# A two-layer hybrid decoder trunk on one core: the norm squares of the dilated blocks move from ScalarE to GpSimd and VectorE

## The chip, the cores and the metric

One core of one Trainium2 chip. The metric is the device time of the whole kernel in microseconds, one launch for both layers. The engines are TensorE (PE, its weight loads PEld), VectorE (DVE), ScalarE (ACT), GpSimd (POOL) and SyncE (SP), which issues the DMAs. Lines named L797 and the like are lines of the kernel before.

## The reference

256 tokens, D_MODEL 1024, two layers. Each layer normalizes x, multiplies it by one wide w_in (1024 rows) and gives parts of the product to three mixers: a latent attention (A), a gated DeltaNet (B) and a dilated window attention (C) with three groups of four heads of 128. Gated branch outputs are projected, merged and put through w_out. The change concerns C, where queries and keys are normalized per head before the rotary embedding:

```python
def rms_norm(x, g):
    xf = x.astype(jnp.float32)
    y = xf * lax.rsqrt(jnp.mean(xf * xf, axis=-1, keepdims=True) + RMS_EPS)
    return (y * g.astype(jnp.float32)).astype(x.dtype)
...
    q, k, v = (t.reshape(B, S, n_heads, DIL_HEAD_DIM) for t in jnp.split(qkv, 3, axis=-1))
    q = apply_rope(rms_norm(q, q_norm_g), cos, sin)
    k = apply_rope(rms_norm(k, k_norm_g), cos, sin)
```

## The kernel before

Everything is float32. Each product with weights is made of three TensorE passes over split operands: high part times high part, high times low, low times high (L797 to L799). The weights come by DMA in pieces of 128x1024 into `raw` (4 slots); ScalarE writes the high part (`prep`, L1119, `w_hi`), VectorE the low part (`prep`, L1446, `w_lo`), into 5 slots each, so that a piece can be made four pieces ahead of its use.

The work is a list of 57 units per layer (`UNITS`, built in `unit_list`), each half of one projection block of 512 columns: 4 row blocks of weights (2 pieces of 2) by 2 token tiles `t` of 128 tokens. A unit's token tile is 12 matmuls of 128x512. Between the units stand all other steps, in one order that is written out by hand (`step_table`, `middle_table`, `build_order`). Each engine walks through this same `ORDER` and emits its own part of each step; an engine's instructions run strictly in that order, and between engines there are only semaphore waits. Behind the second token tile of unit u come its eviction step `("evict", u)`, the steps of `put(u, ...)`, and `prep` of the pieces of unit u + 2.

The dilated blocks are `dil` i = 0 to 8: for group g = i // 3, the queries are i = 3g, the keys 3g + 1, the values 3g + 2. The second halves of the query and key blocks 0, 1, 3, 4, 6, 7 are units 17, 22, 26, 28, 32 and 34. For such a block:

1. TensorE fills two PSUM banks, one per token tile.
2. ScalarE's `evict` (L1121 to L1190) takes each tile: four squares, one per head (L1186, sums of squares into `d_part`), then one scaled copy into the staging tile `stg` (L1189), which frees the bank. `stg` may be overwritten when the rope step of the block before has ended.
3. GpSimd's `d_rs` (L2051) makes the inverse root from the sums.
4. VectorE's `d_rope` (L1787 to L1806) rotates `stg` into `gate`. For keys it first waits until the queries have been transposed out of `gate`, and the other way round.
5. GpSimd's `d_scale` (L2069 to L2075) multiplies `gate` by the roots, two operations of 128x512. The queries of group 0 are not scaled here.
6. TensorE's `tr_step` (L884) transposes the result, four transposes per token tile; ScalarE copies them out (L1362), and scores, softmax and the product with the values follow.

The entries of the order around these steps, shortened:

```python
    put(22, ("dn_cv", 2, 1), ("tr", "dq", 0), ("dn_row", 0), ("dn_row", 1), ("tr", "dq", 1), ("ahead",), ("dn_kk", 0),
        ("d_rs", 0, 1), ("d_rope", 0, 1), ("d_scale", 0, 1), ("dn_th", 2), ("dn_silu", 2))
    put(28, ("pT", 0, 1, 1), ("dn_S", 0), ("d_scale", 1, 0), ("ahead",), ("tr", "dq", 2), ("tr", "dq", 3),
        ("pv", 0, 1, 0), ("d_rs", 1, 1), ("d_rope", 1, 1))
    put(34, ("d_scale", 2, 0), ("dn_S", 6), ("pv", 1, 1, 0), ("tr", "dq", 4), ("tr", "dq", 5), ("ahead",),
        ("d_rs", 2, 1), ("d_rope", 2, 1), ("dn_S", 7), ("d_scale", 2, 1), ("dn_S", 8), ("dn_S", 9))
```

The DeltaNet's steps stand between them: `dn_cv` is its convolution (VectorE, L1556 and L1561), `dn_bT` transposes features, of which VectorE takes the values (L1577) and so frees the banks that the first key transposes (`("tr", "dk", 0)`, L884) use; `dn_decay` is L1593, `dn_S` a row of small operations of the triangular solve (L1630 to L1636).

Of the kernel before, what the change touches and what calls it, by code (L numbers as in the profile page):

```python
# [29 lines left out]
NT = 2  # L30
# [3 lines left out]
H = 4  # L34
# [359 lines left out]
def hybrid_trunk(nc, x, positions, norm_g, w_in, mla_q_a_norm_g, mla_w_q_b, mla_kv_a_norm_g, mla_w_kv_b,  # L394
                 mla_q_norm_g, mla_k_norm_g, dn_conv_w, dn_a_log, dn_dt_bias, dn_out_norm_g,
                 dil_q_norm_g, dil_k_norm_g, w_branch, w_out, tables, out):
    with ExitStack() as ctx:
# [47 lines left out]
        kdec = dnbuf(8)  # L445
        vb = dnbuf(9)

        def narrow(i, a, c):
# [141 lines left out]
        gains_loaded, hi_done, lo_done, piece_done = (sem(k) for k in ("gains_loaded", "hi_done", "lo_done", "piece_done"))  # L590
        roots_moved, sums_moved = sem("roots_moved"), sem("sums_moved")
        z_tanh = [sem(f"z_tanh{t}") for t in range(NT)]
# [48 lines left out]
        def sums_there(layer):  # L641

            return sums_moved, (layer + 1) * (3 * NT * NT * 16)

        def block_taken(u, layer, t=1):

            return taken(bank_unit(u, t), layer)
# [450 lines left out]
        def _(act):  # L1098
# [22 lines left out]
            def evict(step, layer):  # L1121
# [31 lines left out]
                for t in range(NT):  # L1153
# [24 lines left out]
                    elif what == "gate":  # L1178
                        dst, func, scale = gate[:, t, :], ACT.Tanh, hrstd[:, t:t + 1]
                    if what == "dil" and i % 3 < 2:  # L1180

                        if t == 0 and i > 2:
                            act.wait_ge(*after("gpsimd", ("d_rs", i // 3 - 1, i % 3), layer))
                        for h in range(H):
                            c = slice(h * HD, (h + 1) * HD)
                            ins = av(dst[:, c], o[:, c], ACT.Square, scale=scale, accum_out=d_part[d_slot(i)][:, t, h:h + 1])  # L1186
                        own_next(ins, layer)

                    ins = av(dst, o, func, scale=scale)  # L1189
# [238 lines left out]
        def _(dve):  # L1428
# [358 lines left out]
            def d_rope(step, layer):  # L1787

                _, g, k = step
                name = "dq" if k == 0 else "dk"  # L1790
                if g == 0 and k == 0:
                    dve.wait_ge(*after("gpsimd", ("d_tables",), layer))
                else:

                    for j in range(2):
                        dve.wait_ge(*full(("tr", "dq", 2 * g + j) if k else ("tr", "dk", 2 * g - 2 + j), layer))

                dve.wait_ge(*block_taken(unit_of("dil", 3 * g + k) if g + k > 0 else unit_of("branch", GATES[0]), layer))
                s4 = stg.rearrange("p t (h d) -> p t h d", h=H)
                g4 = gate.rearrange("p t (h d) -> p t h d", h=H)  # L1800
                tt(g4, s4, rg[name][0].unsqueeze(2).broadcast_to([P, NT, H, HD]), ALU.mult)
                own_next(tt(s4, s4, rg[name][1].unsqueeze(2).broadcast_to([P, NT, H, HD]), ALU.mult), layer)
                n = HD // 2
                x, v = (b.rearrange("p t (h d) -> p (t h) d", h=H) for b in (gate, stg))
                tt(x[:, :, 0:n], x[:, :, 0:n], v[:, :, n:HD], ALU.add)
                tt(x[:, :, n:HD], x[:, :, n:HD], v[:, :, 0:n], ALU.add).then_inc(part("vector", step), 1)  # L1806
# [105 lines left out]
        def _(pool):  # L1912
# [19 lines left out]
            def evict(step, layer):  # L1932
# [6 lines left out]
                last.then_inc(part("gpsimd", step), 1)  # L1939

            def norm(step, layer):
                pool.wait_ge(*after("scalar", step, layer))
# [108 lines left out]
            def d_rs(step, layer):  # L2051

                _, g, k = step
                i = 3 * g + k
                pool.wait_ge(*block_taken(unit_of("dil", i), layer))
                if i == 0:
# [22 lines left out]
            def prep(step, layer):  # L2079
# [4 lines left out]
                if q != ASIDE:  # L2084
# [4 lines left out]

            parts = {"prep": prep, "evict_branch": evict, "norm": norm, "m_tables": m_tables, "d_tables": d_tables, "lat_norm": lat_norm, "kpe": kpe,  # L2090
                     "q_rs": q_rs, "q_rope": q_rope, "k_rs": k_rs, "dn_gc": dn_gc,
# [25 lines left out]
```

## Time and profile before

| | |
|---|---|
| median of 3 runs | 772.19 us (771.73 to 772.25) |
| profiled execution: time, span | 771.47 us, 769.7 us |
| TensorE busy | 755.1 us (98%) |
| VectorE busy | 584.0 us (76%) |
| ScalarE busy | 475.6 us (62%) |
| GpSimd busy | 179.1 us (23%) |
| DMA | 124.90 MB, mean 162 GB/s |

The span is the time from the first to the last recorded instruction of the profiled execution; its own time has the launch's edges besides. Shares of busy time are averages over the kernel. Timelines give the start and the length of an instruction (or of a run of alike ones), and in brackets how long the engine stood idle before it and what ended that. The second layer repeats the first, 378.7 us later.

### The profile page before, as it was taken

The numbers are of one execution on the slowest core, as the hardware profiler recorded it, in microseconds if no ns is written. First come the engines' busy times: TensorE is split into PE (matmuls) and PEld (weight loads), VectorE is DVE, ScalarE is ACT, GpSimd is POOL, SyncE is SP. The second block draws the span as 40 slices with busy tenths as digits, with TensorE's granted clock in tenths as the row PEclk, the third lists the DMA queues.
The fourth block names the chain that finished last, engine by engine and source line by source line (L and its number), as shares of the span: only waits on it lengthen the run. The fifth ranks groups of instructions, "written<-read, shape, count | busy, mean of one in ns | idle before, by whom it ended". The sixth has DMA issues, their size and how long they took to land.

```text
span 769.7 us, 11699 instructions
## 1 busy us (share of the span) xinstructions
PE 755.1 (98%) x4270; PEld 652.9 (85%) x4270; DVE 584.0 (76%) x844; ACT 475.6 (62%) x1067; POOL 179.1 (23%) x183
## 2 busy tenths in 40 slices
PE   7999999999999999999999999999999999999998
PEld 6999888788887888888899998878888878888886
DVE  6677868988889776776655797789887987667763
ACT  6869585668595654455457768656777856435441
POOL 1165104304231002411032721313050300035100
PEclk9999999999999999999999999999999999999999
DMA  8657636354545445655565564563356545546651
GB/s 244 230 162 219 191 111 188 100 156 138 158 147 180 139 141 169 182 167 192 134 201 179 162 189 136 150 201 115 111 166 163 165 138 164 164 137 191 192 164 55
DMA packets 73039, 124.90 MB, mean 162 GB/s; under 512 B 9757, under 2 KB 17047, under 8 KB 72983
## 3 DMA queue, kind: packets, MB, share of 16 engines
q1 hardware_dynamic: 72560, 124.10, 52.8%
q8 instruction: 34, 0.56, 0.3%
q14 instruction: 22, 0.18, 0.1%
q10 hardware_dynamic: 423, 0.06, 0.0%
HBM read 122.03 MB, written 1.05 MB: 160 GB/s over the span
## 4 chain that ended last, share of the span: by engine, by line
PE 85%; DVE 9%; ACT 3%; issue 2%; DMA 0%; ACTq 0%; DVEq 0%
PE bank L797 22%; PE bank L799 21%; PE bank L798 21%; PE bank L781 3%; PE bank L780 3%; PE bank L779 3%; DVE w_lo L1446 3%; PE bank L937 1%; PE bank L827 1%; PE bank L884 1%; ACT w_hi L1119 1%; PE bank L914 1%; ACT at L1186 1%; PE bank L905 1%; PE bank L932 1%
## 5 line engine op out<-in xcount | busy, mean ns | idle before, releaser
L1446 DVE TENSOR_TENSOR w_lo<-raw,w_hi 128x1024 fp32r<-128x1024 f32 (+4 forms) x240 | 294.8, 1254 | 100.0 <-ACT w_hi L1119 98.5
L1119 ACT ACTIVATE w_hi<-raw 128x1024 fp32r<-128x1024 f32 (+4 forms) x239 | 237.7, 1018 | 76.0 <-PE bank L799 63.8
L797 PE MATMUL bank<-w_hi,hT 128*128 128x512 f32 (+2 forms) x704 | 277.2, 394 | 1.2 <-DVE hT L1497 0.7
L799 PE MATMUL bank<-w_hi,hT 128*128 128x512 f32 (+2 forms) x704 | 270.9, 385 | 0.0
L798 PE MATMUL bank<-w_lo,hT 128*128 128x512 f32 (+2 forms) x704 | 270.5, 384 | 0.0
L797 PEld LDWEIGHTS bank<-w_hi,hT 128*128 128x128 f32 x704 | 132.9, 189 | 26.7 <-DVE hT L1497 1.8
L799 PEld LDWEIGHTS bank<-w_hi,hT 128*128 128x128 f32 x704 | 132.7, 189 | 25.7
L798 PEld LDWEIGHTS bank<-w_lo,hT 128*128 128x128 f32 x704 | 133.0, 189 | 23.2
L1920 POOL TENSOR_TENSOR sm<-sm,tab 128x8 f32<-128x8 f32 (+3 forms) x46 | 53.1, 1155 | 198.0 <-ACT dn L1326 73.2
L1938 POOL TENSOR_TENSOR mixed<-mixed,gate 128x512 f32<-128x512 f32 x12 | 21.1, 1762 | 175.9 <-DVE gate L1467 175.9
L779 PE MATMUL bank<-hT,w_hi 128*128 128x256 f32 x192 | 54.6, 285 | 0.0
L781 PE MATMUL bank<-hT,w_lo 128*128 128x256 f32 x192 | 54.3, 283 | 0.0
L780 PE MATMUL bank<-hT,w_hi 128*128 128x256 f32 x192 | 54.3, 283 | 0.0
L797 PE MATMUL bank<-w_hi,yT 128*128 128x512 f32 (+1 forms) x136 | 53.1, 391 | 1.0 <-ACT gate L1189 0.8
L1189 ACT ACTIVATE at<-bank,sm 128x512 f32<-128x512 f32 (+2 forms) x60 | 38.9, 656 | 23.5 <-PE bank L799 22.7
L799 PE MATMUL bank<-w_hi,yT 128*128 128x512 f32 (+1 forms) x136 | 51.8, 381 | 0.0
L798 PE MATMUL bank<-w_lo,yT 128*128 128x512 f32 (+1 forms) x136 | 51.7, 380 | 0.0
L1381 ACT ACTIVATE at<-at,sm 128x128 f32<-128x128 f32 (+1 forms) x64 | 29.6, 464 | 31.1 <-DVE sm L1767 17.9
L1362 ACT COPY at<-bank 128x512 f32<-128x512 f32 x52 | 29.4, 587 | 22.5 <-PE bank L884 15.6
L2074 POOL TENSOR_TENSOR gate<-gate,sm 128x512 f32<-128x512 f32 x20 | 31.0, 1568 | 39.5 <-DVE gate L1806 39.4
L1186 ACT ACTIVATE at<-bank,sm 128x128 f32<-128x128 f32 x96 | 33.9, 364 | 9.4 <-PE bank L799 8.3
L780 PEld LDWEIGHTS bank<-hT,w_hi 128*128 128x128 f32 x192 | 36.7, 191 | 0.1
(235 smaller groups left out, 991.1 us busy)
## 6 DMA issues: line engine op xcount, KB each, us to landing
raw<-in_w_in SPq DMA_DIRECT2D x168, 512.0 KB, 3.8
raw<-in_w_branch SPq DMA_DIRECT2D x24, 512.0 KB, 4.1
raw<-in_w_out SPq DMA_DIRECT2D x16, 512.0 KB, 4.2
raw<-in_w_in SPq DMA_DIRECT2D x8, 384.0 KB, 4.8
raw<-in_w_in SPq DMA_DIRECT2D x8, 320.0 KB, 4.1
raw<-in_mla_w_kv_b SPq DMA_DIRECT2D x8, 256.0 KB, 2.8
raw<-in_mla_w_q_b SPq DMA_DIRECT2D x4, 384.0 KB, 3.4
xs<-in_x SPq DMA_DIRECT2D x2, 512.0 KB, 4.8
```

Of the source, the lines that this page charges most:

```text
L779: mm(o, hi[:, k, c], src[0][:, a, :], start=first and f == 0, stop=False, skip_group_check=True)
L780: mm(o, hi[:, k, c], src[1][:, a, :], start=False, stop=False, skip_group_check=True)
L781: ins = mm(o, lo[:, k, c], src[0][:, a, :], start=False, stop=last, skip_group_check=True)
L797: mm(o, src[0][:, a, tok], hi[:, k, :], start=starts and p == k == 0, stop=False)
L798: mm(o, src[0][:, a, tok], lo[:, k, :], start=False, stop=False)
L799: last = mm(o, src[1][:, a, tok], hi[:, k, :], start=False, stop=ends(u, p) and k == k1 - k0 - 1)
L1119: av(view(w_hi, q % SPLIT, k1 - k0, n), view(raw, q % RAW, k1 - k0, n), ACT.Copy).then_inc(hi_done, 1)
L1186: ins = av(dst[:, c], o[:, c], ACT.Square, scale=scale, accum_out=d_part[d_slot(i)][:, t, h:h + 1])
L1189: ins = av(dst, o, func, scale=scale)
L1446: tt(view(w_lo, q % SPLIT, k1 - k0, n), view(raw, q % RAW, k1 - k0, n), view(w_hi, q % SPLIT, k1 - k0, n).bitcast(F32), ALU.subtract).then ...
L1920: return tt(dst, src, c.broadcast_to(list(src.shape)), op)
L2074: last = tt(heads(gate[:, t, :]), heads(gate[:, t, :]), per_head(d_root[d_slot(3 * g + k)][:, t, :]), ALU.mult)
```

## The change

ScalarE no longer squares the query and key blocks: its `evict` only copies each tile into `stg`. GpSimd gets a step at the same place in the order (`squares_of`, for the `evict` steps of those six blocks): for each token tile it waits until the copy is made and multiplies the `stg` tile by itself into one of two free 128x512 places of `dn` (`squares`). VectorE sums these by head in two reductions at the head of `d_rope`, ahead of the rotation. `d_rs` then waits for the sums. GpSimd may write the squares of a block when those of the block before have been summed. Two semaphores carry this, `squares_made` and `squares_done`.

```diff
--- before.py
+++ after.py
@@ -444,6 +444,7 @@
         kbg = dnbuf(7)
         kdec = dnbuf(8)
         vb = dnbuf(9)
+        squares = (kbg[:, 0, :], kdec[:, 1, :])
 
         def narrow(i, a, c):
 
@@ -588,7 +589,7 @@
         start = {k: sem(k) for k in ("tab_first", "tab_second", "tab_loaded", "x_loaded0", "x_loaded1", "pos_loaded", "aside_hi", "first_rows", "rows_loaded", "rows_T", "rows_copied",
                                      "angle_step", "angles", "sines", "rot_ready", "stored")}
         gains_loaded, hi_done, lo_done, piece_done = (sem(k) for k in ("gains_loaded", "hi_done", "lo_done", "piece_done"))
-        roots_moved, sums_moved = sem("roots_moved"), sem("sums_moved")
+        roots_moved, sums_moved, squares_made, squares_done = (sem(k) for k in ("roots_moved", "sums_moved", "squares_made", "squares_done"))
         z_tanh = [sem(f"z_tanh{t}") for t in range(NT)]
         own = {e: sem(f"{e}_own") for e in ("vector", "scalar", "gpsimd")}
         seen = dict.fromkeys(own, 0)
@@ -641,6 +642,10 @@
         def sums_there(layer):
 
             return sums_moved, (layer + 1) * (3 * NT * NT * 16)
+
+        def squares_there(i, layer, t=1):
+
+            return squares_done, NT * (layer * 2 * GROUPS + 2 * (i // 3) + i % 3) + t + 1
 
         def block_taken(u, layer, t=1):
 
@@ -1177,15 +1182,6 @@
                         dst, func, scale = z[:, t, :], ACT.Tanh, (hrstd_par if by_parity(u) else hrstd)[:, t:t + 1]
                     elif what == "gate":
                         dst, func, scale = gate[:, t, :], ACT.Tanh, hrstd[:, t:t + 1]
-                    if what == "dil" and i % 3 < 2:
-
-                        if t == 0 and i > 2:
-                            act.wait_ge(*after("gpsimd", ("d_rs", i // 3 - 1, i % 3), layer))
-                        for h in range(H):
-                            c = slice(h * HD, (h + 1) * HD)
-                            ins = av(dst[:, c], o[:, c], ACT.Square, scale=scale, accum_out=d_part[d_slot(i)][:, t, h:h + 1])
-                        own_next(ins, layer)
-
                     ins = av(dst, o, func, scale=scale)
                     ins.then_inc(z_tanh[t] if what == "z" else bank_free[b], 1)
 
@@ -1795,7 +1791,14 @@
                     for j in range(2):
                         dve.wait_ge(*full(("tr", "dq", 2 * g + j) if k else ("tr", "dk", 2 * g - 2 + j), layer))
 
-                dve.wait_ge(*block_taken(unit_of("dil", 3 * g + k) if g + k > 0 else unit_of("branch", GATES[0]), layer))
+                i = 3 * g + k
+                if i > 2:
+                    dve.wait_ge(*after("gpsimd", ("d_rs", g - 1, k), layer))
+                for t in range(NT):
+                    dve.wait_ge(squares_made, squares_there(i, layer, t)[1])
+                    nc.vector.tensor_reduce(d_part[d_slot(i)][:, t, :], heads(squares[t]), AX.X, ALU.add).then_inc(squares_done, 1)
+                if g + k == 0:
+                    dve.wait_ge(*block_taken(unit_of("branch", GATES[0]), layer))
                 s4 = stg.rearrange("p t (h d) -> p t h d", h=H)
                 g4 = gate.rearrange("p t (h d) -> p t h d", h=H)
                 tt(g4, s4, rg[name][0].unsqueeze(2).broadcast_to([P, NT, H, HD]), ALU.mult)
@@ -1938,6 +1941,18 @@
                     last = tt(m, m, gate[:, t, :], ALU.add)
                 last.then_inc(part("gpsimd", step), 1)
 
+            def squares_of(step, layer):
+
+                u = step[1]
+                what, i, hf, nk, n = UNITS[u]
+                if what != "dil" or i % 3 == 2:
+                    return
+                if layer + i > 0:
+                    pool.wait_ge(squares_done, squares_there(i, layer, 0)[1] - 1)
+                for t in range(NT):
+                    pool.wait_ge(*block_taken(u, layer, t))
+                    tt(squares[t], stg[:, t, :], stg[:, t, :], ALU.mult).then_inc(squares_made, 1)
+
             def norm(step, layer):
                 pool.wait_ge(*after("scalar", step, layer))
                 own_next(inverse_root(rstd, ss_x, 1.0 / D, layer), layer)
@@ -2052,7 +2067,7 @@
 
                 _, g, k = step
                 i = 3 * g + k
-                pool.wait_ge(*block_taken(unit_of("dil", i), layer))
+                pool.wait_ge(*squares_there(i, layer))
                 if i == 0:
                     pool.wait_ge(*after("scalar", ("soft", "m", 1), layer))
                 if g > 0:
@@ -2087,7 +2102,7 @@
                 pool.wait_ge(raw_loaded[q % RAW], 16 * RAW_AT[q])
                 nc.gpsimd.tensor_copy(view(w_hi, q % SPLIT, k1 - k0, n), view(raw, q % RAW, k1 - k0, n)).then_inc(start["aside_hi"], 1)
 
-            parts = {"prep": prep, "evict_branch": evict, "norm": norm, "m_tables": m_tables, "d_tables": d_tables, "lat_norm": lat_norm, "kpe": kpe,
+            parts = {"prep": prep, "evict": squares_of, "evict_branch": evict, "norm": norm, "m_tables": m_tables, "d_tables": d_tables, "lat_norm": lat_norm, "kpe": kpe,
                      "q_rs": q_rs, "q_rope": q_rope, "k_rs": k_rs, "dn_gc": dn_gc,
                      "dn_ss": dn_ss,
                      "dn_o": dn_o, "dn_on": dn_on, "d_rs": d_rs, "d_scale": d_scale}
```

How the instructions stand then. Behind a row's shape stand the semaphores that it waits for. Rows of the kernel now have that kernel's line numbers. First GpSimd at the queries of group 1 (steps of units 26 and 28). Before: the root of block 3 (`d_rs`, two rows), its scaling (`d_scale`, two rows of `gate<-gate,sm`), the root of block 4.

```order
L1920 TENSOR_TENSOR sm<-sm,tab 128x2x4 [waits scalar_soft,bank_free3]
L1920 TENSOR_TENSOR sm<-sm,tab 128x2x4 [waits gpsimd_own]
L2074 TENSOR_TENSOR gate<-gate,sm 128x512 [waits vector_d_rope,gpsimd_d_rs]
L2074 TENSOR_TENSOR gate<-gate,sm 128x512
L1929 TENSOR_SCALAR sm<-sm 128x2x4 [waits gpsimd_d_scale,bank_free1]
L1920 TENSOR_TENSOR sm<-sm,tab 128x2x4 [waits gpsimd_own]
```

Now, the same place from the squares of block 3 on (`dn<-at`):

```order
L1954 TENSOR_TENSOR dn<-at 128x512 [waits bank_free2,squares_done]
L1954 TENSOR_TENSOR dn<-at 128x512 [waits bank_free3]
L1923 TENSOR_TENSOR sm<-sm,tab 128x2x4 [waits scalar_soft,squares_done]
L1923 TENSOR_TENSOR sm<-sm,tab 128x2x4 [waits gpsimd_own]
L1954 TENSOR_TENSOR dn<-at 128x512 [waits bank_free0,squares_done]
L1954 TENSOR_TENSOR dn<-at 128x512 [waits bank_free1]
L2089 TENSOR_TENSOR gate<-gate,sm 128x512 [waits vector_d_rope,gpsimd_d_rs]
L2089 TENSOR_TENSOR gate<-gate,sm 128x512
L1932 TENSOR_SCALAR sm<-sm 128x2x4 [waits gpsimd_d_scale,squares_done]
L1923 TENSOR_TENSOR sm<-sm,tab 128x2x4 [waits gpsimd_own]
```

The squares of block 4, which wait for the banks 0 and 1 of unit 28 to be evicted, have come between the root of block 3 and its scaling. At blocks 0, 1, 3 and 6 the squares stand ahead of the block's own root and part no other pair. The squares of block 7 stand in the same way ahead of the scaling of block 6.

VectorE around the rope step of block 0 (unit 21). Before: the DeltaNet's tile (`dn<-bank,sm`), the four rows of the rotation, the next weights, the convolution.

```order
L1588 TENSOR_TENSOR dn<-bank,sm 128x512 [waits bank_full3]
L1801 TENSOR_TENSOR gate<-at 128x1024 [waits bank_free1,gpsimd_d_tables]
L1802 TENSOR_TENSOR at<-at 128x1024
L1805 TENSOR_TENSOR gate<-gate,at 128x8x64 [waits vector_own]
L1806 TENSOR_TENSOR gate<-gate,at 128x8x64
L1446 TENSOR_TENSOR w_lo<-raw,w_hi 128x1024 [waits hi_done] x2
L1556 TENSOR_SCALAR dn<-dn,prm_all 128x256 [waits bank_free3]
```

Now:

```order
L1584 TENSOR_TENSOR dn<-bank,sm 128x512 [waits bank_full3]
L1799 TENSOR_REDUCE sm<-dn 128x4 [waits squares_made,gpsimd_d_tables]
L1799 TENSOR_REDUCE sm<-dn 128x4 [waits squares_made]
L1804 TENSOR_TENSOR gate<-at 128x1024 [waits bank_free1]
L1805 TENSOR_TENSOR at<-at 128x1024
L1808 TENSOR_TENSOR gate<-gate,at 128x8x64 [waits vector_own]
L1809 TENSOR_TENSOR gate<-gate,at 128x8x64
L1442 TENSOR_TENSOR w_lo<-raw,w_hi 128x1024 [waits hi_done] x2
L1552 TENSOR_SCALAR dn<-dn,prm_all 128x256 [waits bank_free3]
```

Two reductions have come ahead of the rotation; the same holds at the other five blocks, and all that follows in VectorE's order stands behind them.

ScalarE at block 4 (unit 28). Before: four squares and a copy for each token tile, a copy of transposed probabilities, the high part of weights.

```order
L1186 ACTIVATE at,sm<-bank,sm 128x128 [waits gpsimd_d_rs,bank_full0,vector_d_rope]
L1186 ACTIVATE at,sm<-bank,sm 128x128 x3
L1189 ACTIVATE at<-bank,sm 128x512 [waits scalar_own]
L1186 ACTIVATE at,sm<-bank,sm 128x128 [waits bank_full1]
L1186 ACTIVATE at,sm<-bank,sm 128x128 x3
L1189 ACTIVATE at<-bank,sm 128x512 [waits scalar_own]
L1362 COPY at<-bank 128x512 [waits bank_full7]
L1119 ACTIVATE w_hi<-raw 128x1024 [waits piece_done,raw_loaded1]
```

Now:

```order
L1185 ACTIVATE at<-bank,sm 128x512 [waits bank_full0,vector_d_rope]
L1185 ACTIVATE at<-bank,sm 128x512 [waits bank_full1]
L1358 COPY at<-bank 128x512 [waits bank_full7]
L1124 ACTIVATE w_hi<-raw 128x1024 [waits piece_done,raw_loaded1]
L1358 COPY at<-bank 128x8x64 [waits bank_full5]
L1358 COPY at<-bank 128x8x64 [waits bank_full6]
```

The copy itself waits for the bank, and what follows it stands eight squares nearer.

## Rows read from the trace of the kernel before

**Rows 1.** The page: engines' busy time in us (share) xinstructions; the granted clock by slice.

```profile
PE 755.1 (98%) x4270; PEld 652.9 (85%) x4270; DVE 584.0 (76%) x844; ACT 475.6 (62%) x1067; POOL 179.1 (23%) x183
...
PEclk9999999999999999999999999999999999999999
```

**Rows 2.** Waits of TensorE: engine line <- waited for: us in total, times, longest.

```profile
PE bank L1075 <- DMA tab<-in_tables: 3.3, 1, 3.3
PE bank L884 <- ACT at L1189: 2.2, 2, 1.1
PE bank L898 <- ACT at L1362: 1.7, 2, 0.9
PE bank L884 <- DVE dn L1577: 1.2, 2, 0.6
...
PE bank L797 <- ACT gate L1189: 0.8, 2, 0.4
```

**Rows 3.** Timeline of ScalarE: start us, us, engine line op out<-in xcount [idle before <-releaser].

```profile
139.02 0.37 ACT L1186 ACTIVATE at<-bank,sm 128x128 f32<-128x128 f32 x1 [0.43 <-PE bank L799]
...
140.56 0.69 ACT L1189 ACTIVATE at<-bank,sm 128x512 f32<-128x512 f32 x1
...
185.53 0.37 ACT L1186 ACTIVATE at<-bank,sm 128x128 f32<-128x128 f32 x1 [0.44 <-PE bank L799]
...
226.15 0.37 ACT L1186 ACTIVATE at<-bank,sm 128x128 f32<-128x128 f32 x1 [0.44 <-PE bank L799]
```

**Rows 4.** Timeline of TensorE.

```profile
141.39 0.63 PE L884 MATMUL bank<-tab,gate 128*128 128x128 f32 x4 [1.10 <-ACT at L1189]
...
157.17 1.07 PE L884 MATMUL bank<-tab,gate 128*128 128x128 f32 x8 [0.58 <-DVE dn L1577]
...
179.78 0.47 PE L797 MATMUL bank<-w_hi,hT 128*128 128x512 f32 x1
...
185.76 1.04 PE L884 MATMUL bank<-tab,gate 128*128 128x128 f32 x8
...
226.84 1.04 PE L884 MATMUL bank<-tab,gate 128*128 128x128 f32 x8
```

**Rows 5.** Groups of VectorE by form: xcount | busy us, mean ns | idle before.

```profile
L1761 DVE TENSOR_REDUCE sm<-at 128x4 f32<-128x512 f32 x8 | 5.4, 680 | 0.2
```

**Rows 6.** Timeline of VectorE, 128 to 157 us.

```profile
128.13 0.69 DVE L1467 SCALAR_TENSOR_TENSOR mixed<-gate,bank 128x512 f32<-128x512 f32 x1 [1.00 <-PE bank L799]
...
131.61 1.21 DVE L1801 TENSOR_TENSOR gate<-at 128x1024 f32<-128x1024 f32 x1
...
143.63 1.23 DVE L1446 TENSOR_TENSOR w_lo<-raw,w_hi 128x1024 fp32r<-128x1024 f32 x1 [0.16 <-ACT w_hi L1119]
144.78 1.22 DVE L1801 TENSOR_TENSOR gate<-at 128x1024 f32<-128x1024 f32 x1
...
149.51 2.06 DVE L1446 TENSOR_TENSOR w_lo<-raw,w_hi 128x1024 fp32r<-128x1024 f32 x1
151.50 2.06 DVE L1593 TENSOR_TENSOR dn<-dn,sm 128x1024 f32<-128x1024 f32 x1
...
155.75 1.28 DVE L1577 TENSOR_TENSOR dn<-bank,sm 128x512 f32<-128x512 f32 x2
```

**Rows 7.** Timeline of GpSimd.

```profile
148.60 3.87 POOL L2074 TENSOR_TENSOR gate<-gate,sm 128x512 f32<-128x512 f32 x2 [4.96 <-DVE gate L1806]
...
180.61 3.59 POOL L2074 TENSOR_TENSOR gate<-gate,sm 128x512 f32<-128x512 f32 x2
...
236.21 2.05 POOL L2074 TENSOR_TENSOR gate<-gate,sm 128x512 f32<-128x512 f32 x2 [4.90 <-DVE gate L1806]
```

**Rows 8.** Timeline of VectorE, 178 to 230 us.

```profile
178.96 2.35 DVE L1446 TENSOR_TENSOR w_lo<-raw,w_hi 128x1024 fp32r<-128x1024 f32 x2
...
181.73 3.55 DVE L1446 TENSOR_TENSOR w_lo<-raw,w_hi 128x1024 fp32r<-128x1024 f32 x2 [0.42 <-ACT w_hi L1119]
...
226.03 3.50 DVE L1446 TENSOR_TENSOR w_lo<-raw,w_hi 128x1024 fp32r<-128x1024 f32 x3
```

## The prediction

> **What bounds the kernel now.** I read the engines' busy shares first: TensorE works in 98% of the span, at a granted clock of full speed (2.4 GHz) in every slice [rows 1]. So time given to or taken from another engine counts only where TensorE waits for it. The list of TensorE's waits is short [rows 2]. Per layer it has a 1.10 us wait for the scalar engine's eviction of a projection block (L884 <- L1189), a 0.87 us wait for a copy of transposed keys (L898), a 0.58 us wait for VectorE (L884 <- L1577) and a 0.41 us wait for a gate's eviction. The rest is the start. The change can give back the 1.10 at most, twice, and it can make waits in TensorE's way wherever GpSimd or VectorE comes late. A difference of 0.2% (1.5 us) is what a measurement of this kernel can tell.
>
> **What leaves ScalarE.** One token tile of a block costs four squares, 139.02 to 140.56, so 1.54 us, ahead of the 0.69 us copy [rows 3]. There are 24 such tiles (6 blocks, 2 tiles, 2 layers): 37 us leave an engine that is 62% busy. Of this, TensorE sees the wait at 141.39 only [rows 4]: it goes, because the copy that frees the bank can start at 139.02. The other evictions release nothing that TensorE waits for.
>
> **What comes on VectorE.** Two reductions of 128x512 to 128x4 stand at the head of each rope step. The same operation on a score tile takes 0.68 us [rows 5], so 1.36 us a block and 16.3 us in all. At two of the six blocks it cannot hide. From 128.13, where VectorE was released by TensorE, to L1577 at 155.75 it has no idle time but 0.16 us [rows 6], and the end of L1577 is what TensorE waits for at 157.17 [rows 4]. The rope steps of blocks 0 and 1 (L1801 at 131.61 and 144.78) lie in this stretch. So 2 x 1.36 - 0.16 = 2.56 us come on L1577.
>
> **What comes on GpSimd.** 24 multiplications of 128x512. Nearest row: the scaling L2074, of the same size, takes 2.05 us for two when VectorE lets it, 3.87 and 3.59 for two when VectorE streams operations with two inputs from SBUF [rows 7]. So 1.03 alone, 1.9 in company. VectorE pays too: beside the 3.87 us pair L1446 and L1593 run from 149.51 to 153.56, 4.05 us [rows 6], where two such operations take 2.35, at 178.96 [rows 8]: 1.70 us lost. Beside the 3.59 pair two L1446 take 3.55 [rows 8]: 1.20 lost. Block 1's second tile can be squared from 139.02 + 0.69 = 139.7 [rows 3] and its first one tile of matmuls sooner, at about 137, while VectorE multiplies convolution taps, two SBUF inputs each. I take 1.70, since those operations are back to back; bounds 0 and 2.1.
> The Trainium skill ("SBUF — State Buffer", section "SBUF: two separate sides") says that a GpSimd operation and a VectorE operation with two SBUF inputs lock each other out for a whole instruction. By that rule a pair would cost 2.1 here in place of 1.70, and the sum 0.8 us more; the trace's stretched rows go the same way.
>
> **Stretch A, TensorE at 157.17:** 2.56 + 1.70 = **4.3 us later** per layer. The 1.10 us gained at 141.39 is lost inside it, as TensorE merely arrives sooner at a wait that VectorE ends.
>
> **Stretch B, unit 28.** L1446 at 178.96 makes the weights of this unit's second piece right behind block 3's rope step. It ends at 180.1, and TensorE, which starts the unit at 179.78 [rows 4], wants it a quarter of the unit later, at about 181.2. With 1.36 us more ahead of it, it comes at 181.5: 0.3 us; bounds 0 and 1.2 (half of a pair's 1.70 ahead of it too).
>
> **The queue of GpSimd.** This is the main term. The squares of block 4 stand on GpSimd ahead of the scaling of block 3's queries (the order rows in the section on the change), and those of block 7 ahead of block 6's. The scaling was done early (180.61 to 184.20 [rows 7]), and TensorE transposes its result at 185.76 without a wait [rows 4]. Now GpSimd must first wait for the second token tile of block 4 to be evicted, and that tile is TensorE's own work until just before the transposes: its first square starts at 185.53 [rows 3], so the copy in its place ends at 186.22. Then come one square (1.03) and the two scalings. Beside them VectorE has one L1446, so 2.05 + 1.17 = 3.2, and 0.2 for the two handovers. TensorE gets its operand at 190.7 instead of 185.76: **4.9 us**. Bounds: all alone, 3.6; all in company, 6.5.
> For block 7 the same chain starts from 226.15 + 0.69 = 226.84 [rows 3]. I put it at 227.1, because block 6's rope step, which must end before block 7 may overwrite the staging tile, is itself late by its reductions and block 6's squares. Then 1.03, and the pair at 3.87, because three L1446 are queued at 226.03 [rows 8], and 0.2: 232.2 against the transposes at 226.84 [rows 4]: **5.4 us**, bounds 3.2 and 6.6.
> Behind each stall ScalarE waits with the copies of the transposes, and behind it the next weights' high part, VectorE's low part and the key block's rope step. These move with TensorE. Since the copies no longer stand behind squares, they save about what the two reductions add, so I count nothing for the waits of 0.87 and 0.41 at the end of the stage; between -0.4 (the last wait goes) and +1.4 (two reductions unhidden). Block 0's squares fall in a stretch where GpSimd is free, and block 3's squares and block 6's delay nothing that TensorE wants within a microsecond.
>
> **Sum.** 4.3 + 0.3 + 4.9 + 5.4 = 14.9 per layer; both layers have the same waits, so 29.7 us. The profiled execution took 771.47 (span 769.7), which gives 801.2; the median of the runs, 772.19, is 0.7 higher: **802**. Bounds per layer: low 2.56 + 0 + 3.6 + 3.2 - 0.4 = 9.0, high 4.7 + 1.2 + 6.5 + 6.6 + 1.4 = 20.4, so 790 to 813.
>
> **Rivals.**
> *The reductions hide (0.20).* VectorE is 76% busy; if its run up to L1577 has slack that I don't see, or the locks cost nothing there, stretch A costs nothing and only the two queue stalls stay: 2 x (4.9 + 5.4 + 0.3) = 21 us, 793. Against it: the unbroken row of starts [rows 6].
> *The clock falls (0.25).* No wait of TensorE in this trace is over 3.3 us [rows 2], and the granted clock reads full speed after each [rows 1]. The new ones are 4 to 6 us. If the clock falls to 1.2 GHz in them and stays there after each for as long as the wait was, half of that time is lost: up to 14.6 us over both layers. If it happens at half of them, 7 us: 809.
> The Trainium skill ("TensorE: Matmul & The Clock Gate", section "Why this matters for your kernels") warns of such a fall when TensorE stands idle for longer than about 3 us between bursts. No wait here decides that.
> *Faster (0.03).* If GpSimd's three operations ended before TensorE came to the transposes, nothing but the relief of ScalarE would be left: two waits of 1.10 and two of 0.41 go, 769. It decides when the last operation ends before 185.76 and 226.84, and the eviction that it must wait for ends later than that by itself.
> *No difference (0.02).* The same with a new wait of 1.5 us per layer for VectorE.
> That the order is not what I say can be ruled out by the order rows; 0.50 is left for the forecast of 802.
>
> **The numbers.** The range holds the forecast's bounds and most of the clock case: 788 to 816. Faster 0.03, same 0.02, slower 0.95.
>
> **What would show it.** In the profile after: no L1186-like squares on ScalarE, and TensorE's wait of 1.10 for ScalarE gone. In the list of TensorE's waits, two waits of 3.6 to 6.5 us per layer for GpSimd's scaling, at the transposes of queries of groups 1 and 2, and one of 4 to 6 us for VectorE's L1577 (0.58 now, plus 4.3, plus the 1.1 by which TensorE comes sooner, of which a part may be waited a step earlier). GpSimd's squares at 1.0 us where VectorE is idle and 1.9 beside it. The granted clock at 1.00 after each wait, or below it, tells the third case. The prediction is wrong if the waits for GpSimd are under 2 us, or if TensorE waits for VectorE no longer than now.

## The result, and the profile after

The changed kernel takes 812.66 us (median of 4 runs, 811.84 to 813.48), the kernel before 771.96 beside it: a ratio of 1.053 (95% interval 1.0515 to 1.054), 40.7 us slower. The profiled execution took 812.62, its span is 810.8 (769.7 before). The forecast was 802, its range 788 to 816.

The page of the kernel after, its lines of busy time, of the clock and of GpSimd's squares:

```profile
PE 769.7 (95%) x4270; PEld 665.5 (82%) x4270; DVE 610.0 (75%) x868; ACT 441.5 (54%) x875; POOL 226.0 (28%) x207
...
PEclk9999999999998999999999999998999899999999
...
L1954 POOL TENSOR_TENSOR dn<-at 128x512 f32<-128x512 f32 x24 | 30.2, 1259 | 117.8 <-ACT at L1185 117.8
```

Against [rows 1] ScalarE has lost 34 us of work, VectorE has 26 more and GpSimd 47 more. TensorE executes the same 4270 instructions and is busy 14.6 us longer: part of its work has become slower. The clock line has three slices with an 8.

TensorE's waits after:

```profile
PE bank L889 <- POOL gate L2089: 18.8, 4, 5.0
PE bank L889 <- DVE dn L1573: 11.1, 2, 5.5
...
PE bank L919 <- ACT at L1358: 1.7, 2, 0.9
```

The 2.2 us for L1189 and the 0.8 for the gate of [rows 2] are gone. The wait for VectorE has grown from 1.2 to 11.1, a wait for GpSimd's scaling has come (18.8), and one for a copy (L919, 1.7).

TensorE's timeline after at the places of [rows 4], and the same engine's granted clock there. The columns of the second are: stretch in us, its length, busy time (number of instructions) of PE, PEld, DVE, ACT and POOL, granted clock, DMA share, GB/s.

```profile
140.69 0.60 PE L889 MATMUL bank<-tab,gate 128*128 128x128 f32 x4
...
161.56 1.94 PE L889 MATMUL bank<-tab,gate 128*128 128x128 f32 x8 [5.53 <-DVE dn L1573]
...
196.92 1.97 PE L889 MATMUL bank<-tab,gate 128*128 128x128 f32 x8 [4.43 <-POOL gate L2089]
...
232.68 0.63 PE L919 MATMUL bank<-tab,at 128*128 128x128 f32 x4 [0.85 <-ACT at L1358]
...
245.54 1.97 PE L889 MATMUL bank<-tab,gate 128*128 128x128 f32 x8 [4.96 <-POOL gate L2089]
```

```profile
158.00:161.00 3.00, 0.00 (x0) 0.00 (x0) 3.00 (x4) 0.00 (x0) 0.00 (x0) 0.62 0.57 160
161.00:166.00 5.00, 4.44 (x23) 4.47 (x24) 2.74 (x4) 2.99 (x7) 0.00 (x0) 0.54 0.76 242
166.00:192.00 26.00, 25.95 (x125) 21.37 (x125) 23.10 (x29) 14.29 (x29) 7.47 (x5) 1.00 0.35 109
...
197.00:200.00 3.00, 3.00 (x17) 3.00 (x17) 1.02 (x2) 1.67 (x3) 0.00 (x0) 0.55 0.60 178
...
245.00:250.00 5.00, 4.46 (x15) 3.88 (x16) 3.17 (x5) 3.04 (x4) 0.49 (x1) 0.50 0.80 247
```

Three things are to be seen. The transposes at 140.69 no longer wait. Each of the three long waits is followed by a stretch at the lower of the two clock levels (1.2 GHz): eight transposes take 1.94 to 1.97 us, where they took 1.04 to 1.07 [rows 4]. The second layer has the same three waits (5.53, 4.44 and 4.96 us), again with 1.94 to 1.97 behind each: six falls in all. And in between, at 166 to 192, the clock is whole.

GpSimd, and the two copies of ScalarE that release it:

```profile
137.91 1.17 POOL L1954 TENSOR_TENSOR dn<-at 128x512 f32<-128x512 f32 x1 [0.71 <-ACT at L1185]
140.34 1.04 POOL L1954 TENSOR_TENSOR dn<-at 128x512 f32<-128x512 f32 x1 [1.26 <-ACT at L1185]
...
192.85 1.04 POOL L1954 TENSOR_TENSOR dn<-at 128x512 f32<-128x512 f32 x1 [0.93 <-ACT at L1185]
193.85 3.02 POOL L2089 TENSOR_TENSOR gate<-gate,sm 128x512 f32<-128x512 f32 x2
...
240.49 1.04 POOL L1954 TENSOR_TENSOR dn<-at 128x512 f32<-128x512 f32 x1 [0.47 <-ACT at L1185]
241.49 4.00 POOL L2089 TENSOR_TENSOR gate<-gate,sm 128x512 f32<-128x512 f32 x2
```

```profile
192.08 0.69 ACT L1185 ACTIVATE at<-bank,sm 128x512 f32<-128x512 f32 x1 [1.98 <-PE bank L804]
...
239.72 0.69 ACT L1185 ACTIVATE at<-bank,sm 128x512 f32<-128x512 f32 x1 [0.89 <-PE bank L804]
```

This is the chain of the forecast (shown for the queries of group 1): TensorE's last matmul of block 4, the copy to 192.77, the square to 193.89, the scaling to 196.87, TensorE at 196.92. Before, the scaling of the same block had been over before TensorE wanted it [rows 7, 4].

VectorE from its release by TensorE to what TensorE waits for, the stretch of [rows 6]:

```profile
128.69 0.69 DVE L1463 SCALAR_TENSOR_TENSOR mixed<-gate,bank 128x512 f32<-128x512 f32 x1 [0.99 <-PE bank L804]
...
132.17 1.27 DVE L1799 TENSOR_REDUCE sm<-dn 128x4 f32<-128x512 f32 x2
...
136.97 3.19 DVE L1442 TENSOR_TENSOR w_lo<-raw,w_hi 128x1024 fp32r<-128x1024 f32 x2
140.09 1.45 DVE L1552 TENSOR_SCALAR dn<-dn,prm_all 128x256 f32<-128x256 f32 x2
...
147.98 1.27 DVE L1799 TENSOR_REDUCE sm<-dn 128x4 f32<-128x512 f32 x2
...
153.91 2.06 DVE L1442 TENSOR_TENSOR w_lo<-raw,w_hi 128x1024 fp32r<-128x1024 f32 x1
155.89 2.06 DVE L1589 TENSOR_TENSOR dn<-dn,sm 128x1024 f32<-128x1024 f32 x1
...
160.14 1.27 DVE L1573 TENSOR_TENSOR dn<-bank,sm 128x512 f32<-128x512 f32 x2
```

There are two pairs of reductions (132.17 and 147.98); the next operation starts 1.19 us behind the first of each, so 2.38 in all. The two L1442 at 136.97 take 3.19 us, where two take 2.35 [rows 8]; GpSimd's square at 137.91 lies beside them. The two L1552 at 140.09 take 1.45, beside the square at 140.34; the same two (L1556 there) took 0.61 before. Each square has thus held VectorE for 0.84 us.

### The profile page after: what moved, and what is told of

The parts are those of the page before. It is cut to its first block, busy times and chain, and to the rows that moved or that the text cites. A ratio compares the mean times of both kernels' runs of the same rounds, so it can differ in the third digit from the quotient of the medians.

```text
span 810.8 us, 11574 instructions
## 1 busy us (share of the span) xinstructions
PE 769.7 (95%) x4270; PEld 665.5 (82%) x4270; DVE 610.0 (75%) x868; ACT 441.5 (54%) x875; POOL 226.0 (28%) x207
## 4 chain that ended last, share of the span: by engine, by line
PE 78%; DVE 13%; issue 3%; ACT 3%; POOL 2%; DMA 1%; SPq 0%; DVEq 0%; ACTq 0%; POOLq 0%
PE bank L802 19%; PE bank L804 19%; PE bank L803 19%; DVE w_lo L1442 3%; PE bank L786 3%; PE bank L785 3%; PE bank L784 3%; PE bank L889 2%; POOL gate L2089 2%; PE bank L832 2%; PE bank L942 1%; DVE sm L1799 1%; DVE at L1805 1%; DVE gate L1804 1%; ACT w_hi L1124 1%
## 5 line engine op out<-in xcount | busy, mean ns | idle before, releaser
L1442 DVE TENSOR_TENSOR w_lo<-raw,w_hi 128x1024 fp32r<-128x1024 f32 (+4 forms) x240 | 296.9, 1262 | 103.3 <-ACT w_hi L1124 101.8
L802 PE MATMUL bank<-w_hi,hT 128*128 128x512 f32 (+2 forms) x704 | 279.3, 397 | 0.4 <-DVE hT L1493 0.3
L802 PEld LDWEIGHTS bank<-w_hi,hT 128*128 128x128 f32 x704 | 134.3, 191 | 26.5 <-DVE hT L1493 1.2
L1923 POOL TENSOR_TENSOR sm<-sm,tab 128x8 f32<-128x8 f32 (+3 forms) x46 | 63.9, 1388 | 122.1 <-ACT dn L1322 37.9
L1954 POOL TENSOR_TENSOR dn<-at 128x512 f32<-128x512 f32 x24 | 30.2, 1259 | 117.8 <-ACT at L1185 117.8
L802 PE MATMUL bank<-w_hi,yT 128*128 128x512 f32 (+1 forms) x136 | 53.2, 391 | 0.2
L889 PE MATMUL bank<-tab,gate 128*128 128x128 f32 x96 | 18.3, 349 | 29.9 <-POOL gate L2089 18.8
L889 PEld LDWEIGHTS bank<-tab,gate 128*128 128x128 f32 x96 | 15.1, 182 | 31.8 <-POOL gate L2089 19.7
```

Source lines behind the costliest of these rows:

```text
L802: mm(o, src[0][:, a, tok], hi[:, k, :], start=starts and p == k == 0, stop=False)
L889: four(step, layer, lambda o, h: tr(o, src(h), ident))
L1442: tt(view(w_lo, q % SPLIT, k1 - k0, n), view(raw, q % RAW, k1 - k0, n), view(w_hi, q % SPLIT, k1 - k0, n).bitcast(F32), ALU.subtract).then ...
L1923: return tt(dst, src, c.broadcast_to(list(src.shape)), op)
L1954: tt(squares[t], stg[:, t, :], stg[:, t, :], ALU.mult).then_inc(squares_made, 1)
```

## The experiments

Times are medians, ratios are to the kernel before, run on the same chip. "L802", "L889" and the like are lines of the changed kernel.

**The order on GpSimd.** Is it the place of the squares, ahead of another block's scaling, or the squares themselves? Here they are called at the head of the block's own `d_rs`.

```diff
+                squares_of(("evict", unit_of("dil", i)), layer)
                 pool.wait_ge(*squares_there(i, layer))
...
-            parts = {"prep": prep, "evict": squares_of, "evict_branch": evict,
+            parts = {"prep": prep, "evict_branch": evict,
...
```

> GpSimd's squares stand at the head of the root step d_rs instead of at the eviction step, so at groups 1 and 2 behind the scaling of the queries; all work is the same. Theory (place in the queue): the two waits of TensorE for the scaling (4.43 and 4.96 us per layer) go, and the falls of the clock behind them; the wait for L1573 (5.53) stays. 812.7 less 2 x (4.4 + 5.0 + 4) is about 786; 784 to 792. Rival (load: the added work itself is too much for GpSimd and VectorE wherever it stands): above 805.

Measured: 792.88 us, ratio 1.028 (1.0264 to 1.0298), just above the expected range. Of the long waits one is left:

```profile
PE bank L889 <- DVE dn L1573: 10.9, 2, 5.4
PE bank L802 <- DVE w_lo L1442: 3.9, 6, 1.1
PE bank L919 <- ACT at L1358: 3.5, 2, 1.7
...
PE bank L889 <- POOL gate L2090: 0.6, 2, 0.3
```

The same work on the same engines, in another place of one engine's order, is worth 19.8 of the 40.7 us, the falls of the clock behind the four waits included. The wait for GpSimd went from 18.8 to 0.6. I had expected 786; of the 7 us missing, 5.7 are longer waits: for VectorE's weights (3.9, none in the changed kernel) and for a copy behind the softmax (3.5, where it had 1.7). I read them as work that the stall of GpSimd had given time to; that is not shown.

**The changed kernel without the sums.** VectorE only signals; the sums are left out of the norms.

```diff
-                    nc.vector.tensor_reduce(d_part[d_slot(i)][:, t, :], heads(squares[t]), AX.X, ALU.add).then_inc(squares_done, 1)
+                    dve.sem_inc(squares_done, 1)
```

> The changed kernel without VectorE's sums of the squares (the norms' sums are left out, GpSimd still squares). Theory: VectorE comes 2.4 us sooner to L1573, so TensorE's wait of 5.53 there falls to about 3.1, perhaps without the fall of the clock (2 us); the two waits for GpSimd's scaling stay above 4. About 803 (800 to 808). Rival (the reductions are the load that costs): below 795.

**The changed kernel without the squares.** GpSimd keeps its waits and signals but multiplies nothing; VectorE reduces another tile instead.

```diff
-                    tt(squares[t], stg[:, t, :], stg[:, t, :], ALU.mult).then_inc(squares_made, 1)
+                    pool.sem_inc(squares_made, 1)
```

> The changed kernel without GpSimd's multiplications: GpSimd waits for the same evictions at the same place and only signals, VectorE reduces another tile of the same size (the squares are left out of the computation). Theory (the queue waits for the eviction of the next block, the square itself is a small part): the waits for the scaling fall by the square's 1.04 us and the lock's part only, to 3.0 to 3.8; the wait for L1573 falls by the 1.66 us that VectorE lost beside the squares, to about 3.9. 812.7 less 2 x (1.7 + 1.2 + 1.2) less some clock: 800 to 806. Rival (the squares' own time on GpSimd is what TensorE waits for): the two waits are gone or under 1 us, below 795.

Measured: 806.94 us without the sums (1.0458, 1.0436 to 1.0479), 793.99 without the squares (1.0286, 1.027 to 1.0301). First TensorE without the sums, then without the squares:

```profile
158.98 1.07 PE L889 MATMUL bank<-tab,gate 128*128 128x128 f32 x8 [3.31 <-DVE dn L1573]
...
192.18 1.97 PE L889 MATMUL bank<-tab,gate 128*128 128x128 f32 x8 [4.43 <-POOL gate L2089]
...
242.59 1.97 PE L889 MATMUL bank<-tab,gate 128*128 128x128 f32 x8 [5.29 <-POOL gate L2089]
```

```profile
159.21 1.09 PE L889 MATMUL bank<-tab,gate 128*128 128x128 f32 x8 [4.10 <-DVE dn L1573]
...
192.49 1.09 PE L889 MATMUL bank<-tab,gate 128*128 128x128 f32 x8 [2.62 <-POOL gate L2089]
...
237.07 1.09 PE L889 MATMUL bank<-tab,gate 128*128 128x128 f32 x8 [3.27 <-POOL gate L2089]
```

"Lock" is here short for the time that VectorE loses beside a square of GpSimd. Stretch A comes apart nearly as the forecast had put it together. Each run must be counted from where it released VectorE at the head of the stretch: 128.13 in the kernel before, 128.69 in the changed one, 128.60 without the sums, 128.04 without the squares. TensorE passes 161.56 - 157.17 = 4.39 later in the changed kernel, of which 0.56 was there at the head: 3.83. The locks alone (without the sums) make it late by 1.81 - 0.47 = 1.34, the sums alone (without the squares) by 2.04 + 0.09 = 2.13. Together that is 3.47; each alone can first use up the 0.16 us in which VectorE was idle [rows 6], and 0.2 stays open. Without the squares the waits for GpSimd are still 2.62 and 3.27: the wait for another unit's eviction, with no arithmetic behind it, is the larger part of each. But that run was 6 us faster than I had expected at least. The reason stands in the rows: behind its waits of 2.62 and 3.27 us the transposes take 1.09, not 1.97, in both layers. So the length of a wait is not all of its price, and the missing time of the changed kernel should be the clock.

**TensorE kept busy in two of the waits.** If it is the clock, it can be held up without touching a wait.

```diff
+                if what == "dq" and i // 2 in APART and t == 0:
+                    pe.wait_ge(*free(step, layer))
+                    for _ in range(10):
+                        mm(ps[banks(step)[0]][:, 0:TAB_FIRST], tab[:, 0:P], tab[:, 0:TAB_FIRST], start=True, stop=True)
```

> The changed kernel with ten extra matmuls of 128x239 on constants (about 4.0 us, results overwritten) ahead of TensorE's wait for the scaled queries of groups 1 and 2. Theory (the clock falls during the long waits and costs 1.4 to 2.7 us after each): the granted clock stays at full speed in and behind these two waits, falls only at the wait for L1573, and the time is 812.7 - 2 x 4.1 = 804 to 806. Rival (the slow rows behind the waits are slow for another reason, the clock is a by-product): 812 to 814; and if the extra matmuls come on top of the wait, 820.

Measured: 805.16 us, ratio 1.0433 (1.0417 to 1.0448): 7.5 us less than the changed kernel, by executing 40 matmuls more (80 by the count of the page, 4350 against 4270, which has each of them twice). The granted clock is 1.00 at 190 to 203 and at 236 to 252 us, and 0.52 at 161 to 167, at the wait that was left as it was.

**And in the third.** The same, with twelve such matmuls ahead of the first key transposes.

```diff
+                if what == "dk" and i == 0:
+                    pe.wait_ge(*free(("dn_qk", 1), layer))
+                    for _ in range(12):
+                        mm(ps[7][:, 0:TAB_FIRST], tab[:, 0:P], tab[:, 0:TAB_FIRST], start=True, stop=True)
```

> The changed kernel with TensorE kept busy in all three long waits: ten matmuls of 128x239 that nothing reads ahead of each wait for the scaled queries of groups 1 and 2 (as in the run before this one of that kind, 805.16 us) and twelve ahead of the wait for VectorE at the first key transposes. Theory: the waits themselves cost what the forecast's steps say, 13.2 us a layer, and the rest of the missing time is the clock, of which the earlier run gave back two of three places. Then the clock stays at 1.00 at 158 to 166 us too, the key transposes take about 1.07 us in place of 1.94, TensorE arrives where it did in the changed kernel, and 2.0 us a layer more come back: 801 us, between 799.5 and 803. Rival: the half rate behind the wait comes from something that starts with the transposes (the operands that arrive late, a burst of loads), and not from the engine standing idle: the time stays at 805 or above, and the transposes stay at 1.9 us.

Measured: 801.56 us, ratio 1.039 (1.0372 to 1.0407). Its stretches behind the three waits, and the key transposes:

```profile
158.00:166.00 8.00, 7.31 (x46) 6.47 (x45) 7.17 (x9) 3.63 (x7) 0.00 (x0) 1.00 0.68 210
190.00:203.00 13.00, 12.60 (x72) 11.06 (x71) 10.47 (x14) 5.18 (x7) 9.51 (x7) 1.00 0.39 133
236.00:252.00 16.00, 15.07 (x77) 13.03 (x76) 14.75 (x20) 6.65 (x9) 9.97 (x7) 1.00 0.47 132
```

```profile
161.21 1.07 PE L897 MATMUL bank<-tab,gate 128*128 128x128 f32 x8 [0.69 <-DVE dn L1581]
```

TensorE gets its operand as late as before (161.21 against 161.56, of which 0.34 is the later start of the stretch, 128.35 against 128.69), but runs at full speed from there, and the page has a 9 in every slice of the clock. The falls of the clock thus cost 812.66 - 801.56 = 11.1 us; counted each from the kernel before that ran beside it, 40.7 - 30.1 = 10.6. With the clock held up the changed kernel takes nearly what the forecast had for its waits alone (30.1 us more than before, for 29.7).

**Without the squares on ScalarE, nothing in their place.** How much could the change have given at best? The kernel before with its squares left out; GpSimd makes its roots of old sums.

```diff
-                    if what == "dil" and i % 3 < 2:
...
-                            ins = av(dst[:, c], o[:, c], ACT.Square, scale=scale, accum_out=d_part[d_slot(i)][:, t, h:h + 1])
-                        own_next(ins, layer)
```

> The kernel before with the squares of the dilated blocks left out altogether (GpSimd takes its roots of old sums): the whole relief of ScalarE and none of the new work. Theory: only the 1.10 us wait per layer goes, and at most the 0.41: 772.0 - 2.2 to - 3.0 = 769.0 to 769.8. Rival (ScalarE's 37 us hide nothing at all that TensorE waits for, the wait moves to another engine): 771.5 to 772.2. Second rival (ScalarE sets more than its rows show): below 765.

Measured: 769.83 us, ratio 0.9975 (0.9966 to 0.9984). TensorE does not wait at 141 us any more, and then:

```profile
157.10 1.06 PE L884 MATMUL bank<-tab,gate 128*128 128x128 f32 x8 [1.73 <-DVE dn L1568]
```

It passes here at 157.10, against 157.17 [rows 4], and this run was 0.18 late at the head of the stretch (128.31): of the 1.10 us it keeps 0.25, the rest is waited for VectorE instead. Leaving out all of ScalarE's squares gives 2.2 us, 0.25%. That this is twice 1.10 is chance: a layer takes 1.0 less (from 157.10 to 534.83, before from 157.17 to 535.89), of which 0.25 is this one and 0.41 the wait for the gate's eviction, which is not in TensorE's list any more.

**The copy ahead of the squares.** The same relief with nothing moved to another engine: in the kernel before, ScalarE copies first, frees the bank, and squares the copy, with a semaphore of its own for `d_rs` and `d_rope`.

```diff
                     ins = av(dst, o, func, scale=scale)
                     ins.then_inc(z_tanh[t] if what == "z" else bank_free[b], 1)
+                    if what == "dil" and i % 3 < 2:
+                        act.wait_ge(*taken(bank_unit(u, t), layer))
...
+                            ins = av(squares[t][:, c], dst[:, c], ACT.Square, accum_out=d_part[d_slot(i)][:, t, h:h + 1])
+                        ins.then_inc(squares_done, 1)
```

> The kernel before, with ScalarE's copy of each tile ahead of its four squares, which then read the staging tile from memory and have a semaphore of their own; all on ScalarE. The bank is free 1.5 us sooner. Theory: the 1.10 us wait per layer goes, what follows on ScalarE is as late as before: 769.6 to 770.4. Rival (the extra wait between copy and squares on ScalarE, and the roots' later start, give the gain back): 771.5 to 773.

Measured: 770.65 us, ratio 0.9983 (0.9974 to 0.9992), just above the expected range: 0.17% faster than the kernel before, and the only version here that computes everything and beats it. The wait moved one step on, to the DeltaNet's matrices, which ScalarE now frees later:

```profile
141.53 0.68 PE L985 MATMUL bank<-dn 128*128 128x128 f32 x4 [0.90 <-ACT at L1366]
```

**What is left once the order is mended.** The new order without the sums, and the new order with block 0 and 1 still squared by ScalarE:

```diff
-                    nc.vector.tensor_reduce(d_part[d_slot(i)][:, t, :], heads(squares[t]), AX.X, ALU.add).then_inc(squares_done, 1)
+                    dve.sem_inc(squares_done, 1)
```

> The kernel with the squares behind the scaling (as in e1_order), without VectorE's sums (left out of the computation). In e1_order TensorE waited for VectorE's weights (L802 <- L1442, 3.9 us in all) and for ScalarE behind VectorE's softmax step (L919, 1.7 us per layer), which the changed kernel did not show. Theory (VectorE is the second bound: once GpSimd's queue no longer holds TensorE, the sums and the locks show): the wait for L1573 falls from 5.4 to about 3.2 and the clock stays up, the waits for the weights go: 792.9 - 2 x (2.2 + 2 + 2) is about 780 (776 to 784). Rival (these waits come from the locks beside GpSimd's squares, the sums hide): 787 or more.

```diff
+                    if what == "dil" and i < 2:
+                        for h in range(H):
+                            c = slice(h * HD, (h + 1) * HD)
+                            ins = av(dst[:, c], o[:, c], ACT.Square, scale=scale, accum_out=d_part[d_slot(i)][:, t, h:h + 1])
+                        own_next(ins, layer)
-                for t in range(NT):
+                for t in range(NT if g else 0):
-                if what != "dil" or i % 3 == 2:
+                if what != "dil" or i % 3 == 2 or i < 3:
```

> The kernel with the squares behind the scaling, and the two blocks of group 0 squared by ScalarE as before; only groups 1 and 2 go by GpSimd and VectorE. Theory (the wait for L1573 is made by the sums of blocks 0 and 1 and the lock beside block 1's squares, all in group 0): that wait is back at 0.6 and its fall of the clock is gone, the waits for the weights at group 2 stay: 792.9 - 2 x (4.9 + 2.0 - 1.1) is about 781 (778 to 784), still above 772. Rival (the wait for L1573 is VectorE's general load): the wait stays above 3, time above 787.

Measured: 782.00 us without the sums (1.0124, 1.0107 to 1.0141), 782.99 with group 0 on ScalarE (1.0142, 1.0127 to 1.0157). The second has no long wait left; TensorE's list of it:

```profile
PE bank L802 <- DVE w_lo L1447: 3.9, 6, 1.1
PE bank L919 <- ACT at L1363: 3.5, 2, 1.8
...
PE bank L889 <- DVE dn L1578: 1.2, 2, 0.6
```

With blocks 0 and 1 back on ScalarE the wait for VectorE is 1.2 us again, as in [rows 2], and 9.9 us of 792.88 are gone. By the runs above it should be 11.3, if stretch A is as long in the new order: stretch A, 3.83 twice, and the clock behind it, 3.6 for both layers (805.16 - 801.56). The rest, 11 us over the kernel before, is groups 1 and 2: VectorE's weights of later pieces come late, and a copy behind the softmax does. These two waits are 7.4 of the 11, and 0.6 is for GpSimd's scaling; for the other 3 I have no row.

The new order without the sums came out within its expected range, but only in part as expected. The copy's wait is back at 0.85 a layer. Of the waits for weights 2.6 of the 3.9 us stay (1.30 in each layer; the other 0.7 of its 3.3 us lies at 20 us, where nothing is changed yet), so the sums are not their only cause; whether the squares are the other was not tried. The wait for L1573 is 3.06 and 3.07, and the clock did fall behind it.

## Why the prediction was right, and where it was short

- *Which engines TensorE waits for, and where*: right. Two waits per layer for the scaling of groups 1 and 2, one for L1577 (now L1573), none for the eviction at 141 us.
- *The queue of GpSimd, 4.9 and 5.4*: measured 4.43 and 4.96. The pair took 3.02 for a forecast of 3.2, and 4.00 for 3.87; the square that the scaling stood behind 1.04 for 1.03. TensorE was late itself by the upstream terms, and block 7's second copy ended at 240.41, 0.08 ahead of the square's start. That the squares must wait for another unit's eviction was the term that decided, as the run with another order shows (19.8 us, the clock included).
- *Stretch A, 4.3*: measured 3.83. The four reductions came at 0.6 us each, not 0.68, as runs of two: 2.38 - 0.16 = 2.22 in place of 2.56. The locks cost 1.68 for a forecast of 1.70, but not where I had put them: one square held the L1442, the other an L1552.
- *The 1.10 us lost inside A*: right but for a quarter: with no squares at all TensorE keeps 0.25 of it.
- *Block 4's weights in stretch B, 0.3*: no wait of TensorE appears there. *End of the stage, 0*: measured +0.85 (L919) - 0.41 (the gate) = 0.44, within its bounds.
- *The sum*: 3.83 + 4.43 + 4.96 + 0.44 = 13.66 per layer for a forecast of 14.9; over both layers 27.3 for 29.7. Held at full clock, the kernel was 30.1 us over the kernel before (801.56 - 771.5). So the waits came out 2.4 us shorter than forecast, and 2.8 us came on top for which I have no row; that 30.1 and 29.7 lie so close is partly luck.
- *The step that fell short is the granted clock.* The forecast counted every wait at its own length, and had the fall as a rival, at 0.25, with 7 us if it came at half of the waits and 14.6 at most. It came at all of them, and cost about 11. So the likeliest case was right on the waits, and the time is that case and the rival together: 802 + 11. The range held the time because it had been drawn over part of that rival, not because the sum had the clock in it. I had the rival's condition in the rows (no wait over 3.3 us before, waits of 4 to 6 after) and should have given it more than half. The Trainium skill ("TensorE: Matmul & The Clock Gate", section "Why this matters for your kernels") warns of idle gaps between bursts of matmuls; the three gaps here, 4.43 to 5.53 us, agree.

The prediction's other rivals fell with the rows: the reductions did not hide, and the lengths 2.62 and 3.27 without any arithmetic show that GpSimd could not have been in time.

## What to carry to other kernels

Work put on an idle engine is paid by what stands behind it in that engine's order: ask what the new instruction waits for before asking what it costs, and place it where its own result is needed, not where its input appears. A relief of an engine that is waited for gives at most those waits, and the next wait behind can take most of even that. Where a change makes TensorE idle for longer than any wait so far, count the wait and then the work behind it at half clock.

## What the runs showed of the hardware

- **The length of a wait alone does not decide whether the clock falls.** In the run without the sums TensorE waits 3.31 us for L1573 in both layers. In the first the clock stays whole and the transposes take 1.07 us (the row at 158.98 above); in the second it falls and they take 1.94:

```profile
553.74 1.94 PE L889 MATMUL bank<-tab,gate 128*128 128x128 f32 x8 [3.31 <-DVE dn L1573]
```

```profile
160.00:162.00 2.00, 2.00 (x18) 1.93 (x17) 1.18 (x3) 1.96 (x6) 0.00 (x0) 1.00 0.51 182
...
554.00:555.00 1.00, 1.00 (x6) 1.00 (x6) 1.00 (x3) 0.13 (x1) 0.00 (x0) 0.50 0.99 326
```

Behind waits of 2.62 us it stayed whole in both layers. Behind the 3.06 us of the new order without the sums it fell, though only after the transposes had begun at speed:

```profile
160.43 1.16 PE L889 MATMUL bank<-tab,gate 128*128 128x128 f32 x8 [3.06 <-DVE dn L1573]
```

```profile
161.00:162.00 1.00, 1.00 (x8) 1.00 (x7) 1.00 (x2) 0.91 (x2) 0.00 (x0) 0.63 0.89 270
```

All waits of 4.10 us and more that stood without matmuls in them were followed by the lower level. What tells the shorter ones apart I can't say from these runs.

- **A square on GpSimd also holds an operation of VectorE with one tensor input.** Two TENSOR_SCALAR of 128x256 float32 (L1552) took 1.45 us beside a square and 0.61 without. The Trainium skill ("SBUF — State Buffer", section "SBUF: two separate sides") names for this lock VectorE operations with two inputs from SBUF and those in a mode that uses both port pairs. The row would fit the second kind; which mode the operation ran in no run here shows. A square cost VectorE 0.84 both times (the squares took 1.17 and 1.04).
- **The first transposes can run at half rate while the clock reads whole.** In the profiled execution after, eight transposes of x took 1.97 us, where the same eight took 1.09 before (at 8.47); the page's clock line shows 9 in that slice in both. The matmuls behind them go on as slowly: 0.47 us each, where the same ones take 0.31 from 12 us on. The 0.56 us by which stretch A begins late are left from there, I take it. No part of the change runs so early, and the run with TensorE busy in two waits, which has all of the change, was at the head of the stretch at 128.18, 0.05 behind the kernel before.

```profile
8.92 1.97 PE L832 MATMUL bank<-tab,xs 128*128 128x128 f32 x8 [0.69 <-DMA xs<-in_x]
...
11.22 0.47 PE L804 MATMUL bank<-w_hi,hT 128*128 128x320 f32 x1
```

- **More work can be faster.** 64 matmuls whose results nothing reads (128 by the page's count, 4398 against 4270) took 11.1 us off the changed kernel's time.
